# Two transformer blocks on one core: block products beside the scan in another order, paced reloads, a weight sum moved to VectorE

## The reference, cut to what matters

```python
h = rmsnorm(x, norm_pre);  proj = h @ w_in
xbc, dt_raw, z_ssd, sc_h, sc_b, sc_c, z_sc = jnp.split(proj, idx, axis=-1)
xbc = jax.nn.silu(causal_dwconv(xbc, ssd_conv_w, ssd_conv_b))
y_ssd = ssd_chunked(xs, dt, a, bm, cm, d_skip)          # 8 chunks of 128 tokens, one state
yz = y_ssd * jax.nn.silu(z_ssd);  y_ssd = rmsnorm(yz, ssd_norm)     # in 2 groups
v = causal_dwconv(sc_c * sc_h, sc_conv_w);  y_sc = sc_b * v * jax.nn.silu(z_sc)
mix = jnp.concatenate([y_ssd, y_sc], axis=-1) @ w_out
```

## Time and profile before

| what | value |
|---|---|
| median of 3 runs | 2533.26 us (2531.26 to 2541.16) |
| the profiled execution | 2538.7 us, of which span 2536.5 us |
| PE busy | 2399.3 us (95%) |
| DVE, ACT, POOL busy | 1569.6, 824.1, 1159.1 us |
| mean granted TensorE clock | 0.975 |

### The profile page before, as it was taken

One profiled execution on the slowest core, in us unless ns is written; L12 is line 12 of the kernel. 1 busy time (PEld: TensorE's weight loads), 2 busy tenths in 40 slices (PEclk: granted clock), 3 DMA queues, 4 the chain that ended last, 5 costly groups with the idle time before them and its releaser, 6 DMA issues.

```text
span 2536.5 us, 33900 instructions
## 1 busy us (share of the span) xinstructions
PE 2399.3 (95%) x12770; PEld 1959.8 (77%) x12770; DVE 1569.6 (62%) x1956; ACT 824.1 (32%) x1209; POOL 1159.1 (46%) x656
## 2 busy tenths in 40 slices
PE   7898999997999899999999999999999999999995
PEld 5686777776888778777878778788877888788885
DVE  6886787875531473123146766755788666777788
ACT  4434535432220121143012222222254333343443
POOL 4565555653343464323322332333464555466661
PEclk9898999998999999999999999999999999999997
DMA  5323333227111322122222212222134454843321
GB/s 202 117 80 117 102 132 108 102 94 290 34 50 50 108 88 85 46 83 91 78 76 76 79 62 74 79 87 91 42 125 150 142 169 147 306 186 143 121 100 67
DMA packets 126655, 277.38 MB, mean 109 GB/s; under 512 B 11713, under 2 KB 56001, under 8 KB 121938
## 3 DMA queue, kind: packets, MB, share of 16 engines
q1 hardware_dynamic: 84256, 214.99, 24.4%
q10 hardware_dynamic: 42290, 60.92, 7.0%
HBM read 199.26 MB, written 76.61 MB: 109 GB/s over the span
## 4 chain that ended last, share of the span: by engine, by line
PE 59%; DVE 8%; issue 4%; DMA 3%; ACT 2%; POOL 2%; ACTq 0%; DVEq 0%; SPq 0%; POOLq 0%
PE pt L2494 30%; PE pt L2951 14%; PE wk L2951 6%; PE pt L2510 1%; DMA eb<-o_d 1%; PE wk L2857 1%; PE wk L2962 1%; DVE eb L2158 1%; PE wk L2827 1%; PE wk L2892 1%; PE wk L2891 1%; POOL xl L699 1%; PE wk L2896 1%; DMA sv_d<-vj 1%; PE wk L2779 0%
## 5 line engine op out<-in xcount | busy, mean ns | idle before, releaser
L663 POOL TENSOR_TENSOR w_hi<-w_raw,ones 128x1024 fp32r<-128x1024 f32 x103 | 199.4, 1936 | 846.4 <-PE pt L2494 779.9
L2494 PE MATMUL pt<-h,w_hi 128*128 128x512 f32 x896 | 290.9, 406 | 1.8 <-ACT cu_o L1220 1.8
L667 POOL TENSOR_TENSOR w_lo<-w_raw,w_hi 128x1024 fp32r<-128x1024 f32 x104 | 282.9, 2720 | 10.0 <-ACT w_hi L840 1.9
L2494 PE MATMUL pt<-l,w_hi 128*128 128x512 f32 x896 | 278.1, 392 | 0.0
L2494 PE MATMUL pt<-h,w_lo 128*128 128x512 f32 x896 | 277.1, 390 | 0.0
L2494 PEld LDWEIGHTS pt<-l,w_hi 128*128 128x128 f32 x896 | 168.8, 188 | 36.7
L2494 PEld LDWEIGHTS pt<-h,w_lo 128*128 128x128 f32 x896 | 168.6, 188 | 36.7
L2494 PEld LDWEIGHTS pt<-h,w_hi 128*128 128x128 f32 x896 | 160.1, 189 | 37.9 <-ACT ebuf L1215 5.3
L725 POOL TENSOR_TENSOR xl<-sraw,xh 128x512 fp32r<-128x512 f32 x80 | 134.1, 1688 | 111.6 <-ACT xh L935 111.6
L782 POOL TENSOR_TENSOR wr_l<-raw,wr_h 128x512 fp32r<-128x512 f32 x80 | 136.4, 1706 | 92.4 <-ACT wr_h L1359 92.4
L2494 PE MATMUL pt<-xh,w_hi 128*128 128x512 f32 x384 | 121.6, 398 | 25.5 <-ACT ea L1108 12.9
(11 more groups left out here) (563 smaller groups left out, 6077.4 us busy)
## 6 DMA issues: line engine op xcount, KB each, us to landing
w_raw<-ws_d SPq DMA_DIRECT2D x106, 512.0 KB, 3.4
fx_d<-stg SPq DMA_DIRECT2D x106, 256.0 KB, 2.8
sraw<-ws_d SPq DMA_DIRECT2D x32, 512.0 KB, 5.6
fraw<-ws_d SPq DMA_DIRECT2D x32, 512.0 KB, 4.8
raw<-ws_d SPq DMA_DIRECT2D x32, 512.0 KB, 8.0
xs0f<-fx_d SPq DMA_DIRECT2D x10, 1024.0 KB, 4.8
xs1f<-fx_d SPq DMA_DIRECT2D x9, 1024.0 KB, 5.0
xs2f<-fx_d SPq DMA_DIRECT2D x9, 1024.0 KB, 4.8
```

Source lines behind the costliest of these rows:

```text
L663: nc.gpsimd.tensor_tensor(out=w_hi[:, u, :], in0=w_raw[:, u, :], in1=zeros, op=ALU.add).then_inc(w_hi_done, 1)
L667: nc.gpsimd.tensor_tensor(out=w_lo[:, u, :], in0=w_raw[:, u, :], in1=w_hi[:, u, :].bitcast(f32), op=ALU.subtract).then_inc(w_split, 1)
L2494: ins = MM(pt[:, slot, h * HALF:(h + 1) * HALF], wt[:, k * P:(k + 1) * P], x[:, k, h * HALF:(h + 1) * HALF], start=first and k == 0 and n ...
```

## The change

Every part of it lies in the first layer, in the three stages described above. POOL's `third_sum` goes, and `weight_sums` on DVE makes it as a third instruction. The waits that count these sums get other numbers. In the convolution stage the differences and their roundings are cut in two halves. In the chunk loop chunk 0 gets an order of its own on ACT and DVE, and chunk 1 gets the order of the later chunks; `decay_rows(j + 1, 0, 8)` goes behind `tanh(j, 2)`. In the last stage the loads are issued at other times, and PE's column sums and `spread` stand around tile 3.

```diff
@@ SP, in chunk 7 of the loop
                 sp.wait_ge(sw_lo, 7 * n + 7)
-                sp.dma_start(sb0_raw[:], ws[S_SB + 4 * C, :, :]).then_inc(w_loaded[0], 16)
-                sp.dma_start(sb1_raw[:], ws[S_SB + 4 * C + 1, :, :]).then_inc(w_loaded[1], 16)
+                sp.dma_start(sb0_raw[:], ws[S_SB + 4 * C, :, :]).then_inc(sc_in[0], 16)
+                sp.dma_start(sb1_raw[:], ws[S_SB + 4 * C + 1, :, :]).then_inc(sc_in[1], 16)
+                sp.wait_ge(sw_lo, SC_PRODUCTS)
+                for u in range(2):
+                    sp.sem_inc(w_loaded[u], 16)
+                    sp.dma_start(w_raw[:, u, :], ws[S_SB + 4 * C + 2 + u, :, :]).then_inc(w_loaded[u], 16)
@@ SP, after the loop
-        for i in range(3):
-            y_load(i)
+        y_load(0)
+        y_load(1)
         sp.wait_ge(sc_prod, SC_PRODUCTS)
         for n, x in enumerate((xh, xl)):
             sp.dma_start(x[:, 0:4, cols(1)].bitcast(f32), x12_d[n, :, :, :]).then_inc(x12_in, 16)
-        sp.wait_ge(sw_lo, SC_PRODUCTS)
-        for u in range(2):
-            sp.wait_ge(w_split, S_SB + 1 + u)
-            sp.dma_start(w_raw[:, u, :], ws[S_SB + 4 * C + 2 + u, :, :]).then_inc(w_loaded[u], 16)
-        y_load(3)
+        y_load(2)
         sp.wait_ge(v_done, 3 * C)
         sp.dma_start(sv_d[C - 1, :, :], vj[:]).then_inc(sv_put, 16)
         sp.wait_ge(sv_put, 16 * (C - 1))
-        v_load(0)
-        y_load(4)
-        v_load(1)
-        for i in range(5, KT):
+        for i in range(3, KT):
+            sp.wait_ge(yz_done, i - 2)
             y_load(i)
             v_load(i - 3)
-        v_load(KT - 3)
-        v_load(KT - 2)
         sp.wait_ge(sv_put, 16 * C)
-        v_load(KT - 1)
+        for i in range(KT - 3, KT):
+            sp.wait_ge(ys_done, i - 4)
+            v_load(i)
@@ POOL, convolution stage
-            if j > 1:
-                for i in range(4 * j - 8, 4 * j - 4):
+            if j > 2:
+                for i in range(*((0, 6), (6, 11), (11, 16))[j - 3]):
                     difference_lo(i)
@@ ACT, convolution stage
-        for i in range(16):
...
-        xbc_pair(1)
+        for u in range(2):
+            xbc_copy(1, u)
+        for i in range(8):
+            difference_hi(i)
+        for u in range(2):
+            xbc_silu(1, u)
...
-        for j in range(2, XBC_T // 2 - 1):
-            xbc_pair(j)
+        for u in range(2):
+            xbc_copy(2, u)
+        for i in range(8, 16):
+            difference_hi(i)
+        for u in range(2):
+            xbc_silu(2, u)
+        xbc_pair(3)
@@ ACT, chunks 1 to 7 (of chunk 0's own order, written out anew, only the head)
+        sc_first(0)
+        sc_hi(4)
         xbc_silu(XBC_T // 2 - 1, 0)
+        sc_hi(5)
+        sc_hi(6)
+        xbc_silu(XBC_T // 2 - 1, 1)
...
             if not last:
                 sc_hi(b + 8)
-                if j:
-                    decay_rows(j + 1, 0, 8)
             sc_11(2 * j + 1)
             tanh(j, 2)
             if not last:
+                decay_rows(j + 1, 0, 8)
                 sc_hi(b + 9)
@@ DVE, convolution stage
+        conv_pair(0)
+        differences(0)
+        differences(1)
         conv_pair(1)
...
+        differences(2)
+        differences(3)
         for j in range(2, XBC_T // 2 - 1):
@@ DVE, weight_sums
             TT(out=sums[:, 0, :], in0=r[:, 1, 0, :], in1=r[:, 1, 1, :], op=ALU.add).then_inc(sw_sum, 1)
-            dve.wait_ge(sw_sum, 2 * n + 1)
+            dve.wait_ge(sw_sum, 3 * n + 1)
             TT(out=sums[:, 1, :], in0=sums[:, 0, :], in1=r[:, 0, 0, :], op=ALU.subtract).then_inc(sw_sum, 1)
+            TT(out=r[:, 1, 0, :], in0=r[:, 0, 0, :], in1=r[:, 1, 0, :], op=ALU.subtract).then_inc(sw_sum, 1)
@@ DVE, chunk 0's own order, from its middle
+        scan_c(0)
+        tap(0, 1)
+        part_u2(1)
+        tap(0, 2)
+        part_x(1)
+        scan_matrix(0)
+        part_22(1)
+        weight_sums(2)
+        part_21(1)
@@ PE, chunk loop
-                if i == (5 if j == 0 else 3 if j == 1 else 1):
+                if i == (1 if j else 5):
                     scan_first(j)
-                if i == (11 if j == 0 else 9 if j == 1 else 8):
+                if i == (8 if j else 11):
                     scan_second(j)
@@ PE, last stage
-        pair(1, S_SB, N_SB, (xh, xl))
+        project(S_SB + 2, N_SB + 1, 0, 0, (xh, xl))
         pe.wait_ge(sq_used, 2 * KT)
         pe.wait_ge(s_ready, C)
         pe.wait_ge(y_evac, C)
         sums(acc_g[:, 0, :], 0)
         sums(acc_g[:, 1, :], 8).then_inc(stat_done, 1)
-        pair(2, S_SB, N_SB, (xh, xl))
+        project(S_SB + 3, N_SB + 2, 1, 1, (xh, xl))
         pe.wait_ge(rstd_done, 3)
         spread(wka, 0)
         spread(wkb, 8).then_inc(spread_done, 1)
+        pair(2, S_SB, N_SB, (xh, xl))
         pair(3, S_SB, N_SB, (xh, xl))
```

More of the change, by code:

```diff
@@ L905, in _, with difference_hi @@
         ins.then_inc(dt_sb, 1)
-        for i in range(16):
+        def difference_hi(i):
             r, c = difference(i)
@@ L1018, in _ @@
         xbc_copy(XBC_T // 2 - 1, 1)
+        sc_first(0)
+        sc_hi(4)
         xbc_silu(XBC_T // 2 - 1, 0)
-        for j in range(C):
+        sc_hi(5)
+        sc_hi(6)
+        xbc_silu(XBC_T // 2 - 1, 1)
+        sc_hi(7)
+        act.wait_ge(xbc_put, 16 * XBC_T)
+        rows_load(0)
+        sc_hi(8)
+        sc_11(0)
+        sc_hi(9)
+        act.wait_ge(adt_done, 1)
+        in_decay(0)
+        state_rows(0)
+        sc_hi(10)
+        decay_rows(0, 0, 8)
+        sc_first(1)
+        sc_hi(11)
+        first_tap(0)
+        decay_rows(0, 8, HEADS)
+        sc_hi(12)
+        decay_exp(0)
+        sc_hi(13)
+        sc_hi(14)
+        tanh(0, 0)
+        tanh(0, 1)
+        sc_hi(15)
+        rows_load(1)
+        sc_11(1)
+        tanh(0, 2)
+        sc_hi(16)
+        tanh(0, 3)
+        for j in range(1, C):
             a, b = 14 * j, 14 * j + 7
             last = j == C - 1
-            if j:
-                sc_hi(a + 3)
+            sc_hi(a + 3)
             sc_first(2 * j)
@@ L1048, in _ @@
             sc_11(2 * j)
-            if j == 0:
-                act.wait_ge(adt_done, 1)
-                in_decay(j)
-                state_rows(j)
             sc_hi(a + 9)
-            if j == 0:
-                decay_rows(j, 0, 8)
             sc_hi(b + 3)
             sc_first(2 * j + 1)
-            if j == 0:
-                decay_rows(j, 8, HEADS)
             first_tap(j)
-            if j == 0:
-                decay_exp(j)
             sc_hi(b + 4)
             sc_hi(b + 5)
-            if j and not last:
+            if not last:
                 rows_load(j + 1)
@@ L1080, in _ @@
             if not last:
+                decay_rows(j + 1, 0, 8)
                 sc_hi(b + 9)
-                if j:
-                    decay_rows(j + 1, 8, HEADS)
-                else:
-                    rows_load(j + 1)
+                decay_rows(j + 1, 8, HEADS)
             tanh(j, 3)
@@ L1615, in conv_pair, with differences @@
                         ins.then_inc(conv_done, 1)
-        conv_pair(0)
-        for k in range(4):
+        def differences(k):
             for m in range(4):
@@ L1809, in gate_branch @@
             TT(out=vj[:, cols(h)], in0=vj[:, cols(h)], in1=(s22, su2)[h][:], op=ALU.mult).then_inc(v_done, 1)
-        for j in range(C):
+        part_u2(0)
+        weight_sums(1)
+        part_x(0)
+        part_22(0)
+        part_21(0)
+        product_half(0, 0)
+        scan_input(0)
+        scan_decayed(0)
+        part_12(0)
+        product_half(0, 1)
+        scan_c(0)
[7 more added lines that the diff above has]
+        part_21(1)
+        gate_z(0, 1)
+        gate_z(0, 0)
+        scan_out(0)
+        gate_branch(0, 0)
+        scan_state(0)
+        part_12(1)
+        gate_branch(0, 1)
+        for j in range(1, C):
             a, b = 2 * j, 2 * j + 1
@@ L1845, in _ @@
                 weight_sums(b + 1)
[L1846 to L1849 removed]
+            scan_out(j)
             part_x(b)
[L1851 to L1854 removed]
+            scan_state(j)
             part_22(b)
[L1856 to L1857 removed]
+            gate_z(j, 1)
             part_21(b)
[L1859 to L1860 removed]
             gate_z(j, 0)
[L1862 to L1863 removed]
             gate_branch(j, 0)
[L1865 to L1866 removed]
             part_12(b)
```

83 lines of the change are left out of this document (17 added, 66 removed).

## The result

The changed kernel takes **2542.88 us** (median of 14 runs), the kernel before 2532.77 in runs on the same chips: ratio 1.0036, 95% interval 1.0027 to 1.0046. By the ratio it is slower by 9 us (the medians differ by 10.1), where I had forecast 2.5 us less. The forecast took 0.5% as the least that can be told from no change; the interval here is 0.1% on either side. The profiled execution is 2542.65 us (span 2540.9). PE is busy for as long as before; its waits have changed places.

What follows compares the result with a forecast made beforehand. PE, busy for 95% of the span, was taken to bound the kernel, so only its idle stretches and slow clock could give time. Terms -3.5 - 5.2 - 2.3 + 1 + 7.5 = -2.5 us gave 2530.8 by the median; range 2520 to 2544.

Steps and rivals of the forecast that it cites:

- no change: Whole kernel: the case of a time within 0.5%, or 12.7 us, of the kernel before; chance 0.60.
- Convolution stage: Up to product 4 of chunk 0: PE's wait moves from tile 4 to tile 8; -3.5 us, bounds -15.2 and +3.
- I follow DVE instruction by instruction: Convolution stage: differences doubled where POOL works, lone length elsewhere; DVE's pair 2 ends at 149.5.
- The strict reading of the Trainium skill: Convolution stage: every two-input DVE instruction waits out one of POOL's; pair 2 ends near 155, term 0 instead of -3.5.
- Chunk 0: Chunk 0: part_x no longer waits behind weight sums and scan_matrix, product 11 starts 8 to 11 us early; -5.2 us.
- the step that took y_evac to come 11 us early: Chunk 0: y_evac 11 us early, SP's loads behind it; PE waits about 2.4 us at scan_first of chunk 1.
- Chunk 1 and the later turns: Chunk 1 -2.3, five later turns +1: tanh waits go, part_x late by 0.7 at product 0, 2.3 at product 4.
- My first rival: Later turns: part_x is in time and the tanh waits go whole; -15.4 in place of +1, 2514.5 us; chance 0.18.
- Last stage: Last stage: tile 2 starts 6.9 us early, but PE waits at column sums (7.8) and spread (9.2); +7.5 us.
- the term for the clock: Last stage: 0.4 us for PE's slower clock, added to 7.1 us of longer waits.
- my slower rival: Last stage: paced y loads become the chain if one takes over 7.1 us to land; +15.0, 2548 us; chance 0.14.
- That the change does little: Convolution stage and chunk 0: DVE holds both, PE waits as long elsewhere, -3.5 and -5.2 fall away; 2539.5 us; chance 0.12.

Runs made afterwards that it cites:

- experiment 6: Changed kernel with POOL's sixteen difference_lo all behind its last weight split of the convolution stage; 2540.7 us, ratio 1.0038.
- experiment 1: Changed kernel with PE's order of the last stage put back, paced loads kept; 2525.76 us, ratio 0.9969.
- experiment 2: Changed kernel with only the spread put back behind tile 5, column sums still ahead of tile 3; 2533.03 us, ratio 0.9997.
- experiment 9: Changed kernel with ACT's silu of tile 9 one weight rounding earlier, ahead of the one that waits for POOL's fourth sum; 2536.65 us, ratio 1.0014.
- experiment 3: Changed kernel with the third weight sum back on POOL; 2526.71 us, ratio 0.9977.
- experiment 4: Changed kernel with the third sum still on VectorE but behind part_x in every chunk; 2533.83 us, ratio 0.9995.
- experiment 5: Kernel before with only the first eight decay_rows moved behind the third tanh, from chunk 1 on; 2518.81 us, ratio 0.9941.
- the combined: Changed kernel with PE's old last-stage order, third sum on POOL, copies of tiles 6 and 7 each behind its own buffer's reader; 2511.57 us, ratio 0.9914.

## Why the prediction was wrong, step by step

The measured time lies inside the range and in the case "no change", but on the other side of zero. The sum was -2.5; by the same landmarks it is +8.8, 11.3 more. Three terms carry the difference.

**Convolution stage: -3.5 forecast, +0.5 measured; the step "I follow DVE instruction by instruction" failed.** The place was right: the wait left tile 4 and stood at tile 8. But DVE ended pair 2 at 154.4, not 149.5. I doubled the differences beside POOL and left the dt chain at its length of before, 11.8 us; the chain had POOL's weight splits and differences beside it now, and eight of its fourteen small instructions waited out one of POOL's, 18.7 us in all, and 10.7 with most of POOL's work out of the way (experiment 6). The strict reading of the Trainium skill (SBUF — State Buffer, Who interferes with whom), one engine holds the shared ports for its whole instruction, gave an end near 155 and a term of 0 in the forecast. The trace agrees with it: 154.4 and +0.5. Five of the eight stretched instructions read only one tensor, though, and my sentence on the rule spoke of two.

**Chunk 0: -5.2 forecast, +0.5 measured (-1.5 to -2.2 by experiments 1, 2 and 6); what failed is the step that took y_evac to come 11 us early.** SP's first issue behind the wait for it (timelines of SP: kernel before, changed kernel, experiment 9):

```profile
237.13 0.38 SPq L489 DMA_DIRECT2D ys_d<-yb  x1
...
237.23 0.38 SPq L489 DMA_DIRECT2D ys_d<-yb  x1
...
228.19 0.38 SPq L489 DMA_DIRECT2D ys_d<-yb  x1
```

It came no earlier than before. The wait for part_x did go, and scan_second's wait is 0.66, in the forecast's 0.5 to 1.6. What I did not cost is that ACT's silu of tile 9 had been put behind a rounding that waits for POOL's fourth sum. In the changed kernel (timelines of ACT and of SP):

```profile
191.76 0.63 ACT L935 ACTIVATE xh<-sraw 128x512 fp32r<-128x512 f32 x1 [3.25 <-POOL sraw L730]
192.30 1.04 ACT L875 ACTIVATE sil<-conv_o 128x1024 f32<-128x1024 f32 x1
...
198.29 0.38 SPq L473 DMA_DIRECT2D st<-xbc_d  x1
```

The store, then ACT's and SP's loads, then scan_first follow: a wait of 7.0 (5.3 to 5.5 in experiments 1, 2 and 6) and half clock behind it. With that one line back chunk 0 is 8.0 us shorter than before (51.1 against 59.1, experiment 9), so the gain was there to be had, and the late store took it back. A moved step with a DMA behind it has to be followed to the DMA's reader.

**Chunk 1 and the later turns: -2.3 and +1 forecast, -3.2 and +0.3 measured; right, by the mechanism named.** The tanh waits went, part_x came late by 2.0 (forecast 2.3) and a turn stayed at 48.0 (47.8). The reason was right too: experiments 3, 4 and 5 put the price of the third sum at 2.5 us a turn, 1.9 of it for standing ahead of part_x. The 0.7 at product 0 did not come. My first rival, tanh waits going whole, is what happens without that sum, and experiment 5 measured 14.6 for it, on the kernel before, where I had 15.4.

**Last stage: +7.5 forecast, +10.8 measured; the mechanism is right, the term for the clock was mis-sized.** Tile 2 starts 5.7 us early by this stage (forecast 6.9), the sums wait 7.1 (7.8), the spread 8.8 (9.2): 23.05 us of waits, 23.1 forecast. A slip of 0.7 is in it: 35.4 us from 588.4 end at 623.8, not at 624.5, which makes the wait at the sums 7.1. But I gave 0.4 for the clock, and 3.8 are left when 7.0 of waits are taken from 10.8. In this stage PE works 21.7 us at 1.2 GHz in the changed kernel and 14.2 in the kernel before; half of the 7.5 more is lost, 3.8. Three waits of 7 to 9 us cost more clock than one of 12.9 and one of 3.1.

**The paced loads** did not become the chain (my slower rival): a gated step takes 3.0 to 4.2 us, never over 5, and no wait of DVE there ends with a y load. They seem to have paid their way: tile 2 is 4.8 to 5.7 us earlier by this stage in experiment 1 and in the changed kernel. No run has the paced loads alone, so this is read from the traces and not shown by a run. **That the change does little** is nearest in outcome, 2539.5 against 2542.9, and its reason held for the convolution stage alone.

## What to carry to other kernels

Cost every line of a bundle by itself: here two edits gave some 20 us (decay_rows moved, 14.6 in a run of its own; loads paced, some 5 by the traces) and two took 33 back (the sums and spread moved forward on PE, 17; the third sum on VectorE, 16), and the bundle as a whole shows only 9. Before a reduction or a broadcast is moved forward on PE, look up when its input is made, and leave it behind as much work as that takes. Where VectorE and GpSimd work side by side, count a tiny VectorE instruction that reads only SBUF at the length of the GpSimd one it can meet (eight of fourteen met one here).

## What the runs showed of the hardware that I had not expected

- VectorE instructions of 0.17 to 0.29 us, one of them on 128x16 elements, take 1.0 to 2.5 us beside POOL in the changed kernel's dt chain, and end 0.1 to 0.2 us behind POOL's instruction. Those that read one operand from PSUM (part_x and its like, 80 in the changed kernel, 0.68 to 0.69 us each, 41 of them with POOL at work) are not stretched.
- The store of tile 9 (512 KB) lands in 2.6 us in six of the profiled executions, in 3.3 to 3.5 in six others, and in 4.7 and 4.9 in the combined and the changed kernel. It is not the order of the program alone: experiments 1, 2 and 6 have the changed kernel's order there and 3.3 us. What makes the difference stays open.
- A wait of 7 us ahead of scan_first cost 2.9 us more between there and scan_second, at the lower clock; those of 5.3 to 5.5 in experiments 1, 2 and 6 cost 1.7 to 2.6, and one of 1.3 us nothing (18.9 us, with the full clock granted throughout).
